# Four rearrangements in a fused two-block kernel: a later forget panel, longer tails for the last heads, squares in two parts, four units per tile

## The reference, cut to what matters

```python
# first block
h = rms_norm(x, w) * (1 + scale) + shift            # scale, shift, gate from silu(c) @ ada_w
u, g_pool, q, f_pre, i, g_h = split(h @ w_in)       # six sections of 1024 columns
d = windowed_mean(u, w=2,4,8,16) - u                # four groups of 256 channels
pool_out = (d @ pool_w) * pool_scale * silu(g_pool)
f = lb + (1 - lb) * sigmoid(f_pre);  k = 1 - f      # 8 heads of 128
o = hgrn2(q, log f, k, v=i)                         # gated linear attention with decays
o = rms_norm(o, nw) * silu(g_h)                     # mean of squares over the 128 of a head
y = concat(pool_out, o) @ w_out
x2 = x + gate * rms_norm(y, post_w)
# second block: h = rms_norm(x2, norm_g); proj = h @ w_in_2; four branches
# (spatial gating, top-k sparse latent attention, gated convolution, forgetting attention),
# gated sum, merged @ w_out, final rms_norm
```

## Time and profile before

| | |
|---|---|
| median of three runs | 1144.36 us |
| the profiled execution | 1144.1 us |
| its span | 1142.4 us |
| granted clock of PE, mean | 0.998 of 2.4 GHz |
| PE / DVE / ACT / POOL busy | 98% / 57% / 40% / 4% |

### The profile page before, as it was taken

One profiled execution on the slowest core, in us unless ns is written; L12 is line 12 of the kernel. 1 busy time (PEld: TensorE's weight loads), 2 busy tenths in 40 slices (PEclk: granted clock), 3 DMA queues, 4 the chain that ended last, 5 costly groups with the idle time before them and its releaser, 6 DMA issues. The chain is left out here.

```text
span 1142.4 us, 16726 instructions
## 1 busy us (share of the span) xinstructions
PE 1123.7 (98%) x6872; PEld 920.1 (81%) x6872; DVE 646.6 (57%) x1036; ACT 460.9 (40%) x755; POOL 43.3 (4%) x47
## 2 busy tenths in 40 slices
PE   8999999999999999999999999999999999999997
PEld 8888878878887887878888788877788888888886
DVE  6875766955565246457789893446454344334433
ACT  6472344233675235543342433335542222223233
POOL 1000112300001000000000000000000000000000
PEclk9999999999999999999999999999999999999999
DMA  9543233332215322412223232221122322232211
GB/s 372 200 148 120 76 115 127 121 93 77 74 56 170 115 81 72 154 69 81 86 74 94 73 97 81 81 75 60 52 92 94 110 92 92 93 111 93 93 56 74
DMA packets 32541, 116.83 MB, mean 102 GB/s; under 512 B 3776, under 2 KB 3776, under 8 KB 32464
## 3 DMA queue, kind: packets, MB, share of 16 engines
q1 hardware_dynamic: 30672, 109.88, 29.3%
q0 software_dynamic: 1648, 5.83, 1.5%
q10 hardware_dynamic: 144, 0.03, 0.0%
HBM read 113.64 MB, written 2.10 MB: 101 GB/s over the span
## 5 line engine op out<-in xcount | busy, mean ns | idle before, releaser
L1041 DVE TENSOR_TENSOR w_lo<-raw,w_hi 128x1024 fp32r<-128x1024 f32 (+2 forms) x181 | 224.7, 1243 | 269.2 <-ACT w_hi L584 267.5
L1587 PE MATMUL acc<-hT_hi,w_hi 128*128 128x512 f32 x904 | 361.3, 400 | 0.4 <-DVE hT_lo L1027 0.4
L1589 PE MATMUL acc<-hT_hi,w_lo 128*128 128x512 f32 x904 | 352.5, 390 | 0.0
L1588 PE MATMUL acc<-hT_lo,w_hi 128*128 128x512 f32 x904 | 352.0, 389 | 0.0
L584 ACT ACTIVATE w_hi<-raw 128x1024 fp32r<-128x1024 f32 (+2 forms) x181 | 187.4, 1037 | 131.9 <-PE acc L1589 130.2
L1587 PEld LDWEIGHTS acc<-hT_hi,w_hi 128*128 128x128 f32 x904 | 169.9, 188 | 38.7 <-issue 5.1
L1589 PEld LDWEIGHTS acc<-hT_hi,w_lo 128*128 128x128 f32 x904 | 169.7, 188 | 36.2
L1588 PEld LDWEIGHTS acc<-hT_lo,w_hi 128*128 128x128 f32 x904 | 170.0, 188 | 34.5 <-issue 1.4
L1587 PE MATMUL acc<-w_hi,hT_hi 128*128 128x512 f32 (+1 forms) x160 | 63.6, 397 | 2.8 <-DVE silu_out L1109 2.3
L1589 PE MATMUL acc<-w_hi,hT_lo 128*128 128x512 f32 (+1 forms) x160 | 61.8, 386 | 0.0
L1588 PE MATMUL acc<-w_lo,hT_hi 128*128 128x512 f32 (+1 forms) x160 | 61.6, 385 | 0.0
(11 more groups left out here) (356 smaller groups left out, 1584.8 us busy)
## 6 DMA issues: line engine op xcount, KB each, us to landing
raw<-in_ga SPq DMA_DIRECT2D x32, 512.0 KB, 3.4
ada_raw<-in_ada SPq DMA_DIRECT2D x16, 512.0 KB, 11.7
raw<-in_wo SPq DMA_DIRECT2D x16, 512.0 KB, 3.6
raw<-in_br SPq DMA_DIRECT2D x16, 512.0 KB, 3.4
raw<-in_q SPq DMA_DIRECT2D x8, 512.0 KB, 3.6
raw<-in_u SPq DMA_DIRECT2D x8, 512.0 KB, 3.7
raw<-in_gp SPq DMA_DIRECT2D x8, 512.0 KB, 4.4
raw<-in_ada_w SPq DMA_DIRECT2D x8, 512.0 KB, 3.7
```

What stands on the lines that cost most here:

```text
L1041: nc.vector.tensor_tensor(out=w_lo[:, k % SPLITS, 0:width], in0=raw[:, n % RING, 0:width], in1=w_hi[:, k % SPLITS, 0:width].bitcast(f32), ...
L1587: nc.tensor.matmul(ps, w[0], x[0], start=first, stop=False)
L1588: nc.tensor.matmul(ps, w[0], x[1], start=False, stop=False)
L1589: return nc.tensor.matmul(ps, w[1], x[0], start=False, stop=last)
```

## The change

It has five parts.

1. `f` 7 moves from before `q` 0 to before `pw` 1. `GATES_AT` and `DIFF_AT` now list where gates and differences are made: heads 0 to 6 in `q` 0 to `q` 3, head 7 in `pw` 1; the fourth difference moves from `gp` 7 to `i` 1. The levels of the second group come later: after `u` 6, `gp` 6, `i` 0, `i` 2, `pw` 3, `i` 4, `i` 5, `i` 6 instead of after `pw` 2, `u` 7, `gp` 7, `i` 1, `i` 3, `i` 4, `i` 5, `i` 6.
2. The squares are summed as two fp32r matmuls, of a rounded half `sq_hi` and a rest `sq_lo`. DVE makes both in `split_squares`, ahead of `chain_states` in its queue. `head_mean_squares` comes at the third block of the panel instead of the second.
3. `HEAD_AT` gets `wo` 1 as number 9. Sums of squares of heads 6 and 7 are made in `wo` 0 and `wo` 1 after their first token tile (six matmuls). GpSimd's loads of x and of three rows wait for the last of these sums instead of the last output.
4. `wo` 12 to 15 are multiplied together, 24 matmuls for each tile. `bs` 0 gets split buffers of its own (`first_hi`, `first_lo`); in the entry's order tile 2's first half moves ahead of `upper_h2(0)` on ACT and `lower_h2(0)` on DVE, and tile 2's norm ahead of `bs` 2's split.
5. In a slot without new scores both sums come after the first turn, so the last such slot goes turn, sum, sum, turn instead of turn, sum, turn, sum.

```diff
-ORDER += [("f", 7)] + [("q", j) for j in range(6)]
+ORDER += [("q", j) for j in range(6)]
...
-    ORDER += {0: [("q", 6)], 1: [], 2: [("q", 7)], 3: [("i", j) for j in range(4)]}[g] + [("pw", g)]
+    ORDER += {0: [("q", 6)], 1: [("f", 7)], 2: [("q", 7)], 3: [("i", j) for j in range(4)]}[g] + [("pw", g)]
...
+GATES_AT = {("q", 0): [0, 1], ("q", 1): [2, 3], ("q", 2): [4, 5], ("q", 3): [6], ("pw", 1): [7]}
+DIFF_AT = {("gp", 1): 0, ("gp", 3): 1, ("gp", 5): 2, ("i", 1): 3}
...
-LEVEL_AT = {USED[_first + n]: m for m, n in enumerate([*range(0, 16, 2), 18, 20, 22, 24, 26, 28, 29, 30])}
+LEVEL_AT = {USED[_first + n]: m for m, n in enumerate([*range(0, 16, 2), 20, 22, 24, 26, 28, 29, 30, 31])}
...
-HEAD_AT = {u: n for n, u in enumerate([("gh", j) for j in range(8)] + [("wo", 0)])}
+HEAD_AT = {u: n for n, u in enumerate([("gh", j) for j in range(8)] + [("wo", 0), ("wo", 1)])}
...
-TOGETHER = {("wo", 15): 3, ("bs", 2): 3, ("w2", 7): 2}
+TOGETHER = {("wo", 15): 4, ("bs", 2): 3, ("w2", 7): 2}
...
+        sq_hi = at("sq_hi", R_H, [P, S], f32r)
+        sq_lo = at("sq_lo", R_H + 2048, [P, S], f32r)
...
+        def split_at(k):
+
+            if USED[k] == ("bs", 0):
+                return first_hi[:, :], first_lo[:, :]
+            return w_hi[:, k % SPLITS, :], w_lo[:, k % SPLITS, :]
...
-            pool.wait_ge(o_made, HEADS)
+            pool.wait_ge(ms_made, HEADS)
...
                 rstd_of_y(1)
                 rstd_of_x2(1)
+                square_y(2)
+                rstd_of_y(2)
                 upper_h2(0)
                 split_hi(STEP["bs", 1])
-                square_y(2)
-                rstd_of_y(2)
+                rstd_of_x2(2)
                 split_hi(STEP["bs", 2])
                 upper_h2(1)
-                rstd_of_x2(2)
...
+            def split_squares(n):
+
+                dve.wait_ge(sq_made, n + 1)
+                if n:
+                    dve.wait_ge(ms_made, n)
+                nc.vector.tensor_copy(sq_hi[:, :], o_sq[:, :]).then_inc(sq_hi_made, 1)
+                dve.wait_ge(sq_hi_made, n + 1)
+                nc.vector.tensor_tensor(out=sq_lo[:, :], in0=o_sq[:, :], in1=sq_hi[:, :].bitcast(f32), op=ALU.subtract)\
+                    .then_inc(sq_lo_made, 1)
...
                 norm_x2(1)
+                make_x2(2)
                 lower_h2(0)
                 split_lo(STEP["bs", 1])
-                make_x2(2)
+                norm_x2(2)
                 split_lo(STEP["bs", 2])
                 lower_h2(1)
-                norm_x2(2)
...
-                    if kt == 1 and early is not None:
+                    if kt == 2 and early is not None:
                         early()
...
+                            if early is not None and (t, a) == (1, 0):
+                                early()
...
                 pe.wait_ge(o_squared, n + 1)
-                nc.tensor.matmul(side[3][:, :], ones[:, :], o_sq[:, :], start=True, stop=True).then_inc(ms_made, 1)
+                pe.wait_ge(sq_lo_made, n + 1)
+                nc.tensor.matmul(side[3][:, :], ones[:, :].bitcast(f32r), sq_hi[:, :], start=True, stop=False)
+                nc.tensor.matmul(side[3][:, :], ones[:, :].bitcast(f32r), sq_lo[:, :], start=False, stop=True).then_inc(ms_made, 1)
...
-                    if i < len(sums_):
+                    if not scores_ and i == 0:
+                        for s in sums_:
+                            sum_values(s)
+                    if scores_ and i < len(sums_):
                         sum_values(sums_[i])
...
-                if head == HEADS:
-                    head_mean_squares(HEADS - 2)
...
-                if head == HEADS:
-                    head_mean_squares(HEADS - 1)
```

More of the change, by code:

```diff
@@ L581, in split_hi @@
                 act.wait_ge(raw_in[n % RING], 16 * (n // RING + 1))
-                if k >= SPLITS:
+                if k >= SPLITS and (kind, j) != ("bs", 0):
                     act.wait_ge(unit_used, k - SPLITS + 1)
-                nc.scalar.activation(w_hi[:, k % SPLITS, 0:width], raw[:, n % RING, 0:width], ACT.Copy)\
+                nc.scalar.activation(split_at(k)[0][:, 0:width], raw[:, n % RING, 0:width], ACT.Copy)\
                     .then_inc(hi_made, 1)
@@ L725, in upper_parts @@
             def upper_parts(kind, j, n):
-                done_head = HEADS - 1 if (kind, j) == ("wo", 1) else n - 2 if n else -1
+                done_head = n - 2 if n else -1
                 if done_head >= 0:
@@ L787, in _ @@
                 before = kind
-                if (kind, j % 2) == ("gp", 1):
-                    g = j // 2
+                g = DIFF_AT.get((kind, j))
+                if g is not None:
                     act.wait_ge(d_made, g + 1)
@@ L793, in _ @@
                     nc.scalar.activation(d_hi[:, :, :], sums[(g + 1) % 2][:, :, 0:S], ACT.Copy).then_inc(d_hi_made, 1)
-                for h in gates_in(k):
+                for h in GATES_AT.get((kind, j), []):
                     act.wait_ge(f_bound, h + 1)
@@ L843, in _ @@
                             .then_inc(freed["act"], 1)
-                if n:
+                if n in range(1, HEADS + 1):
                     act.wait_ge(o_made, n)
@@ L847, in _ @@
                         act.wait_ge(mixh_made, n - 1)
-                    nc.scalar.activation(o_sq[:, :], side[3][:, :], ACT.Square)
+                    nc.scalar.activation(o_sq[:, :], side[3][:, :], ACT.Square).then_inc(sq_made, 1)
                     nc.scalar.activation(o_sb[:, :], side[3][:, :], ACT.Copy).then_inc(o_squared, 1)
-                if n == HEADS:
-                    rstd_of_head(HEADS - 1)
                 if (kind, j) == ("wo", 7):
@@ L1040, in split_lo @@
                 dve.wait_ge(hi_made, k + 1)
-                nc.vector.tensor_tensor(out=w_lo[:, k % SPLITS, 0:width], in0=raw[:, n % RING, 0:width],
-                                        in1=w_hi[:, k % SPLITS, 0:width].bitcast(f32), op=ALU.subtract).then_inc(lo_made, 1)
+                hi, lo = split_at(k)
+                nc.vector.tensor_tensor(out=lo[:, 0:width], in0=raw[:, n % RING, 0:width],
+                                        in1=hi[:, 0:width].bitcast(f32), op=ALU.subtract).then_inc(lo_made, 1)
             def total_of(half, heads):
@@ L1322, in _ @@
                 before = (kind, j)
-                if (kind, j % 2) == ("gp", 1):
-                    g, w = j // 2, 2 << (j // 2)
+                g = DIFF_AT.get((kind, j))
+                if g is not None:
+                    w = 2 << g
                     total, diff = sums[g % 2], sums[(g + 1) % 2][:, :, 0:S]
@@ L1380, in _ @@
                 n = HEAD_AT.get((kind, j))
-                if n is not None:
-                    if n < HEADS:
-                        chain_states(n)
-                    if n == HEADS:
-                        finish_head(HEADS - 1)
+                if n in range(1, HEADS + 1):
+                    split_squares(n - 1)
+                if n in range(HEADS):
+                    chain_states(n)
                 if (kind, j) == ("wo", 10):
@@ L1577, in weights @@
                     pe.wait_ge(lo_made, k + 1)
-                return w_hi[:, k % SPLITS, :], w_lo[:, k % SPLITS, :]
+                return split_at(k)
             def bank(result):
@@ L1603, in panel, with token_units @@
                 ins.then_inc(unit_used, 1)
-            def token_units(k, kind, j, source, width, x_ready=None, tile_done=None):
+            def token_units(k, kind, j, source, width, x_ready=None, tile_done=None, early=None):
                 per, count = TOKEN_UNITS[kind], TOGETHER.get((kind, j), 1)
@@ L1924, in _ @@
                     token_units(k, kind, j, mixed_tile, S,
-                                tile_done=(lambda t: transpose_x2(t - 2) if t >= 2 else None) if j == 15 else None)
+                                tile_done=(lambda t: transpose_x2(t - 2) if t >= 2 else None) if j == 15 else None,
+                                early=(lambda: head_mean_squares(head - 2)) if head is not None else None)
                 if (kind, j) in LEVEL_AT:
                     level_scores(LEVEL_AT[kind, j])
-                if head:
+                if head in range(1, HEADS + 1):
                     head_output(head - 1)
```

15 lines of the change are left out of this document (7 added, 8 removed).

## The result

The changed kernel takes 1135.47 us (median of five runs, 1135.22 to 1135.83). Beside the 1144.36 of before that is a ratio of 0.992 (95% interval 0.9907 to 0.9934), 8.9 us less where 10.9 were forecast. The profiled execution took 1135.34 with a span of 1133.6, so by spans the gain is 8.8.

A forecast was written before the change was run, and what follows sets the result against it. PE, busy 98% and in order, bounds the kernel: its work plus its stops. Gains 2.2 + 2.0 + 1.85 + 2.2 + 1.8 + 0.85 = 10.9 us gave 1133.5 us, range 1131.7 to 1137.2.

The forecast's parts named there:

- A: Sums of squares: DVE's copy for `sq_hi` takes full length, gain 0.7 + 1.5 us instead of 4.2, time 1135.5; chance 0.17.
- C: Entry not helped, since the chain through ACT and DVE has hardly any slack; 1134.3 to 1135.3 us; chance 0.08.
- D: Heads: DVE, given 1.1 us more work a panel, becomes the bound and the kernel gets slower; chance 0.02.
- E: Whole kernel: no difference, the stops only move as each engine waits for the next; chance 0.03.
- B: DVE stays behind in `i` 0: 0.9 us less gain, or 2.2 if the whole stop stays; 1134.4 to 1135.7; chance 0.15.
- Part 4: Later levels and fourth difference: PE's stop in `i` 0 for the bank of `gp` 7 shrinks to 0.35, 2.2 us gained.
- Parts 1 and 2: Sums of squares as two fp32r matmuls, placed later: 2.2 us gained in `gh` 2 to 7, 2.0 in `wo` 0 and 1.
- Part 3: `f` 7 moved before `pw` 1: PE's stop there for `d_lo` goes, 1.85 us gained.
- Part 5: Entry, after `wo` 12 to 15: tiles complete earlier, a stop of 0.3 is left of 2.1, 1.8 us gained.
- Part 6: Last sums: the second sum lies beside ACT's copy, for which PE waits 0.84; 0.85 us gained.

## Why the prediction came out as it did

The frame held: PE's stream of starts with its stops sets the time, each stop that went was gained whole, and none came up elsewhere except at one place in `i` 1. Rivals A, C, D and E did not occur. B did, DVE's slowness beside POOL as it said, though the big widening that it also named took its usual 2.28; the totals it did not name. The stop stayed at 1.97 of its 2.54, and with the place in `i` 1 that comes to 2.0 less gain than forecast, close to the 2.2 at which B put a stop that stays whole. A had the same price, 1135.5, so the time alone could not have told the two apart; the rows do.

**Part 4, the term that was wrong: 2.2 forecast, 0.2 measured.** The step that failed is "widening level 8, its copy and the totals: 11.1 to 18.3, the end of it beside POOL", and with it the way in which DVE's time beside POOL was taken, as double. Counted from `pw` 2's start (195.09) the widening came at 11.1 as reckoned (206.17), and POOL began at 16.0, as reckoned. But the totals ended at 24.6 instead of 18.3, and the product of `gp` 7 at 33.3 instead of 31.64, with PE there at 31.5. Doubling is what a large operation shows (2.28 becomes 4.02, in the earlier trace rows). A small one does not double: it waits for a whole operation of POOL, and 0.29, 0.23 and 0.19 became 1.92, 1.92 and 1.94. Doubling over POOL's 8.6 us would have cost DVE 4.3; four small ones in a row cost it 7.3. That this overlap is the cause is shown by moving POOL's work alone (2.25 gained by medians, the wait gone). Moving DVE's work (2.7 gained) agrees, but there PE also came later to the bank. The other half of the reasoning held: taking the difference out of `gp` 7 is worth 2.7 by starts, and the 3.3 of its run hold a stretch at the lower clock besides.

The Trainium skill (SBUF — State Buffer, Who interferes with whom) says that the two lock each other out for a whole instruction. The runs agree, with 0.29 becoming 1.92. The bound that the prediction drew from it, hardly a thing done until 27.2 and 1.3 gained, was still too good. It took 5.4 us of DVE's queue as left when POOL ended at 27.2. POOL, hardly held up by small operations, ended at 24.6 already, but from there to the product's end at 33.3 it was 8.7 us, since two splits of `w_lo`, the gate of `gp` 6, the widening and a third split all came after the totals.

**Part 4, the rest.** The place in `i` 1 took back another 0.25 to 0.35. It stands in the changed kernel and, as a wait of "issue", in some of the experiments with the same code there, of 0.2 to 0.5 by starts. It is absent in the three runs in which DVE was in time at `i` 0, and all but absent in three in which DVE was late there (three units together, the last sums alternating, the difference back in `gp` 7). No row names what PE waited for, so its cause stays open.

**Parts 1 and 2: 4.2 forecast, 3.8 measured.** The copy took 0.43, so A fell. PE was just in time for the matmul, as reckoned, and the late weight load cost 0.16 a sum instead of 0.1; the run with the sums later took that away. What the prediction did not ask is whether the chosen place was right. One block later in the panels and one tile later in `wo` cost nothing and gave 2.7.

**Part 3: 1.85 forecast, 1.81 measured.** Undone, it gave 1.9 back, 1.7 of it by starts at this place.

**Part 5: 1.8 forecast, 2.2 measured.** The walk through the queues left 0.3 at tile 3 and took 2.1 as the price of the old stops, which by starts cost 2.2. No stop is left in the entry; tile 3's norm was done at 450.51, right at PE's transposes at 450.57.

**Part 6: 0.85 forecast, 0.89 measured.** The stop is gone, and its undoing put 0.84 back in the slot.

## What to carry to other kernels

Before work is moved on DVE, look at what POOL does at its new time, and count operations, not microseconds: of a row of small two-input operations each that falls under POOL's cost about one operation of POOL here. Where a new dependency is just in time by hundredths, price the place one block later too, if nothing needs the result yet. And in a kernel bound by one in-order engine, a walk through the other queues from one fixed zero is worth its trouble: five of six terms came within 0.4 us.

## What the runs showed of the hardware

DVE's small additions beside POOL's back-to-back sums: on 128, 64 and 32 columns 1.92, 1.92 and 1.94 instead of 0.29, 0.23 and 0.19. The operation on 8 columns took 2.42 instead of 0.17 in one trace; in seven others it found the gap between two of POOL's and kept its 0.17. POOL's operations took 2.14 each. Beside large operations of DVE the same POOL operations took 3.09 each. A weight load released too late for its matmul cost 0.16 a sum without any wait of PE in the list, seen only in starts 0.31 apart instead of 0.23. A float32 matmul of 512 columns by `ones` cost 0.86 to 0.93 in the stream, and two fp32r matmuls 0.47. In the one trace in which PE stood for 4.7 us in `i` 0, its granted clock was 0.50 of 2.4 GHz from 231.79 to 235.20, which cost 1.3; stops of 2.54 and less left it at 1.00.
